# Gate and up projections as 2x2 block products: seven block products in place of eight, with weight sums on GpSimd

## The reference, cut to what matters

```python
x = x + concatenate([o_a, o_r]) @ w_out            # 1024 x 1024
h = rms_norm(x, g_ffn)
x = x + (silu(h @ w_gate) * (h @ w_up)) @ w_down   # 1024 x 2816, 1024 x 2816, 2816 x 1024
```

## Time and profile before

| what | value |
|---|---|
| median of 3 runs | 1565.37 us (1564.64 to 1566.42) |
| the profiled execution, its own time | 1564.63 us |
| its span, first to last instruction | 1563.1 us |
| PE busy | 1526.0 us (98%) |
| DVE busy | 737.0 us (47%) |
| ACT busy | 480.4 us (31%) |
| POOL busy | 43.3 us (3%) |
| mean granted TensorE clock | 0.998 |

### The profile page before, as it was taken

One profiled execution on the slowest core, in us unless ns is written; L12 is line 12 of the kernel. 1 busy time (PEld: TensorE's weight loads), 2 busy tenths in 40 slices (PEclk: granted clock), 3 DMA queues, 4 the chain that ended last, 5 costly groups with the idle time before them and its releaser, 6 DMA issues.

```text
span 1563.1 us, 29251 instructions
## 1 busy us (share of the span) xinstructions
PE 1526.0 (98%) x11565; PEld 1472.5 (94%) x11565; DVE 737.0 (47%) x1314; ACT 480.4 (31%) x740; POOL 43.3 (3%) x83
## 2 busy tenths in 40 slices
PE   6999999999999999999989999999999999999998
PEld 5998889999999999999989988898999999999998
DVE  5347754754444224443252777467544432344422
ACT  4233453443222112222232245434322221122211
POOL 1001100000000000000010010000000000000000
PEclk9999999999999999999999999999999999999999
DMA  5423321222223322223242133122222232222331
GB/s 175 118 68 106 93 62 58 71 80 79 81 81 96 93 60 86 83 86 93 64 136 82 55 123 91 42 67 81 73 81 81 81 107 73 77 81 81 96 91 62
DMA packets 220383, 132.50 MB, mean 85 GB/s; under 512 B 4424, under 2 KB 213504, under 8 KB 220304
## 3 DMA queue, kind: packets, MB, share of 16 engines
q1 hardware_dynamic: 215200, 114.11, 24.9%
q0 software_dynamic: 5008, 17.29, 3.6%
q10 hardware_dynamic: 96, 0.02, 0.0%
HBM read 123.23 MB, written 8.18 MB: 84 GB/s over the span
## 4 chain that ended last, share of the span: by engine, by line
PE 94%; DVE 3%; issue 2%; ACT 1%; DMA 0%; DVEq 0%; SPq 0%; ACTq 0%
PE ps L1134 70%; PE ps L1255 13%; PE ps L1309 2%; PE ps L1401 1%; PE ps L1416 1%; PE ps L1351 1%; PE ps L1331 1%; PE ps L1200 1%; PE ps L1180 1%; PE ps L1440 1%; DVE sc L905 0%; PE ps L1316 0%; DMA stage<-in_x_sample 0%; PE ps L1451 0%; DVE mix L923 0%
## 5 line engine op out<-in xcount | busy, mean ns | idle before, releaser
L1134 PE MATMUL ps<-ffn,w_hi 128*128 128x288 f32 x2816 | 489.7, 296 | 0.0
L1134 PEld LDWEIGHTS ps<-ffn,w_hi 128*128 128x128 f32 x2816 | 414.4, 189 | 0.2
L709 DVE TENSOR_TENSOR w_lo<-w_raw,w_hi 128x1024 fp32r<-128x1024 f32 (+1 forms) x192 | 247.7, 1290 | 171.6 <-ACT w_hi L439 171.6
L439 ACT ACTIVATE w_hi<-w_raw 128x1024 fp32r<-128x1024 f32 (+1 forms) x192 | 211.8, 1103 | 311.9 <-PE ps L1134 293.6
L1134 PE MATMUL ps<-ffn,w_lo 128*128 128x288 f32 x1408 | 301.6, 296 | 0.0
L1134 PE MATMUL ps<-act,w_hi 128*128 128x288 f32 x1408 | 244.6, 296 | 0.0
L1134 PE MATMUL ps<-mix,w_hi 128*128 128x288 f32 x1280 | 226.5, 300 | 12.1 <-DVE mix L723 10.2
L1134 PEld LDWEIGHTS ps<-ffn,w_lo 128*128 128x128 f32 x1408 | 226.9, 189 | 0.0
L1255 PE MATMUL ps<-mix,w_hi 128*128 128x288 f32 x1024 | 211.4, 300 | 0.0
L1134 PEld LDWEIGHTS ps<-act,w_hi 128*128 128x128 f32 x1408 | 207.3, 189 | 0.0
L1134 PEld LDWEIGHTS ps<-mix,w_hi 128*128 128x128 f32 x1280 | 190.8, 192 | 14.3 <-DVE mix L723 10.6
(11 more groups left out here) (183 smaller groups left out, 1113.1 us busy)
## 6 DMA issues: line engine op xcount, KB each, us to landing
w_raw<-in_w_in SPq DMA_DIRECT2D x56, 512.0 KB, 3.7
w_raw<-in_w_gate SPq DMA_DIRECT2D x44, 512.0 KB, 3.8
w_raw<-in_w_up SPq DMA_DIRECT2D x44, 512.0 KB, 3.8
w_raw<-in_w_down SPq DMA_DIRECT2D x32, 704.0 KB, 4.5
w_raw<-in_w_out SPq DMA_DIRECT2D x16, 512.0 KB, 3.6
strip_even<-bias_lines POOLq DMA_DIRECT2D x8, 320.0 KB, 4.4
strip_odd<-bias_lines POOLq DMA_DIRECT2D x8, 320.0 KB, 5.1
stage<-in_x_prompt SPq DMA_DIRECT2D x2, 1024.0 KB, 6.8
```

The lines of the kernel that those rows point to most:

```text
L439: nc.scalar.activation(w_hi[:, slot, 0:k, :], w_raw[:, slot, 0:k, :], ACT.Copy).then_inc(hi_done, 1)
L709: nc.vector.tensor_tensor(w_lo[:, slot, 0:k, :], w_raw[:, slot, 0:k, :], w_hi[:, slot, 0:k, :].bitcast(F32), ALU.subtract).then_inc(lo_don ...
L1134: last = nc.tensor.matmul(ps[:, bank + half, 0:HALF], w[:, slot, k, :], src[:, k, part, HALF * half:HALF * half + HALF], start=k == 0 and ...
```

## The change

The gate and up weights of block f form a 2x2 block matrix: rows gate and up, columns the two halves of the depth (4 blocks of 128 each). The activations form the other one: the two depth halves by the two token halves. Winograd's form of Strassen's method gets the four result blocks from seven block products: of A11, A12, A22 and four sums S1 to S4 of weight blocks, with B11, B21, B22 and four sums T1 to T4 of activation blocks. A block product is 4 depth blocks x 3 passes = 12 matmuls of 288 columns into one bank.

What each engine now does for one block f (a "pair"):

- SP loads both weights into `pair_raw` (two slots).
- POOL makes S1 = A21+A22, S2 = S1-A11, S3 = A11-A21, S4 = A12-S2 (`weight_sums`), each 128x512.
- ACT makes the high parts and DVE the low parts of the seven factors, each 128x512 (`factor_hi`, `factor_lo`). Each factor has a single place in SBUF; its next high part is made once its product is done (`follow`).
- PE runs the seven products in the order A11, A22 (of the pair before), S2, S1, A12, S3, S4. Some are added to what already lies in their bank.
- Between products ACT and DVE take partial sums out of PSUM: `product_1`, `made_15`, `made_16`, then the corners `corner_11`, `corner_12`, `corner_21`, `corner_22`. The products are not scaled one by one: `scale_gate` and `scale_up` use 576 columns.

In the layer's transition from `w_out`, the activation blocks and their sums are made and split (`operand`, `operand_sums`, `operand_lo`, `sum_lo`). The down units and the first part of the layer keep their work; buffers are placed anew.

The core of the diff (the helpers that only count are left out):

```diff
-        w_raw = place("w_raw", [P, RING, FT, P], F32, A_W)
-        w_hi = place("w_hi", [P, RING, FT, P], F32R, A_W + RING * UNIT)
-        w_lo = place("w_lo", [P, RING, FT, P], F32R, A_W + 2 * RING * UNIT)
+        FACTORS = ("A11", "S2", "S1", "A12", "S3", "S4")
...
+        BANK_1, BANK_5, BANK_6 = 4, 5, (3, 0)
+        FIRST_PAIR = ("A11", "S1", "A12", "S2", "S4", "S3")
+        STEPS = ("A11", "A22", "S2", "S1", "A12", "S3", "S4")
+        FACTOR_OF = {"A11": "B11", "A12": "B21", "A22": "T4", "S1": "T1", "S2": "T2", "S3": "T3", "S4": "B22"}
...
 (POOL)
+                        wait_apart(pool, (pair_loaded[n.par], pair_count(l, g, n)))
+                        free("S1", "S2")
+                        nc.gpsimd.tensor_tensor(w_sum["S1"][:], a21, a22, ALU.add).then_inc(w_summed, 1)
+                        wait_apart(pool, (w_summed, summed + n.count(4, 1)))
+                        nc.gpsimd.tensor_tensor(w_sum["S2"][:], w_sum["S1"][:], a11, ALU.subtract).then_inc(w_summed, 1)
+                        free("S3", "S4")
+                        nc.gpsimd.tensor_tensor(w_sum["S3"][:], a11, a21, ALU.subtract).then_inc(w_summed, 1)
+                        wait_apart(pool, (w_summed, summed + n.count(4, 2)))
+                        nc.gpsimd.tensor_tensor(w_sum["S4"][:], a12, w_sum["S2"][:], ALU.subtract).then_inc(w_summed, 1)
...
 (DVE; free() above waits for the low part of the last pair's factor of that name)
-                    with dve.Fori(1, FT - 1) as f:
-                        group_lo(2 * f + 1, 1)
-                        scaled(U_LAYER * l + 2 * f + first, 0, work[:, 0, :])
-                        act_low(f - 1)
-                        group_lo(2 * f + 2, 0)
-                        up_out(f)
-                        product(f)
+                    def steps(n):
+                        scale_gate(n.prev())
+                        follow(n, "A11")
+                        corner_21(n.prev())
+                        follow(n, "A22")
+                        made_16(n)
+                        follow(n, "S2")
+                        gate_up(n.prev())
+                        made_15(n)
+                        follow(n, "S1")
+                        scale_up(n.prev())
+                        follow(n, "A12")
+                        corner_22(n)
+                        follow(n, "S3")
+                        act_low(n.prev())
+                        corner_12(n)
+                        follow(n, "S4")
...
 (PE)
+                        for k in range(KH):
+                            for i, (w, part) in enumerate(PASSES):
+                                last = nc.tensor.matmul(ps[:, bank, 0:HALF], (f_hi, f_lo)[w][name][:, k, :], tile[:, at, k, part, :],
+                                                        start=start and k + i == 0,
+                                                        stop=k == KH - 1 and i == 2, skip_group_check=True)
+                        last.then_inc(products, 1)
...
+                    def steps(n, after_first=False):
+                        old, bank = n.prev(), BANK_6[n.par]
+                        product(n, "A11", n.at("A11"), BANK_1, True, (c11_out, done(n, 0)))
+                        corner_product(old, n.at("A22"))
+                        waits = [] if after_first else [(c21_made, done(n, -1))]
+                        product(n, "S2", n.at("S2"), bank, True, *waits)
+                        product(n, "S1", n.at("S1"), BANK_5, True, (c12_made, done(n, 0)))
+                        product(n, "A12", n.at("A12"), BANK_1, False, (p1_out, done(n, 1)))
+                        product(n, "S3", n.at("S3"), bank, False, (p16_made, done(n, 1)))
+                        product(n, "S4", n.at("S4"), BANK_5, False, (p15_made, done(n, 1)))
```

More of the change, by code:

```diff
@@ L684, in _, with follow @@
-                    with eng.Fori(1, FT - 1) as f:
-                        gate_up(f)
-                    silu(FT - 1)
-                    group_hi(DOWN, 0, FT)
-                    act_high(FT - 1)
-                    group_hi(DOWN + 1, 1, FT)
+                        sum_hi(2, slice(0, KH), 2 * KH)
+                    corner_11(first)
+                    def follow(n, name):
+                        m = n if name == "A22" else n.next()
+                        free = None if n.first and name == "A22" else (products, made + n.at(name) + 1)
+                        factor_hi(g, m, name, free)
@@ new lines, in corner_22, with corner_21 @@
+                    def corner_22(n):
+                        product_done(n, "S3")
+                        ours(p15_made, n)
+                        if not n.first:
+                            ours(act_f, n, 0)
+                        nc.vector.tensor_tensor(work[:, 1, HALF:TOK], ps[:, BANK_6[n.par], 0:HALF], p15_f[:], ALU.add).then_inc(c22_made, 1)
+                    def corner_21(n):
+                        dve.wait_ge(products, made + (n.next().at("A22") + 1 if n is not LAST else G_PROD))
+                        nc.vector.tensor_tensor(work[:, 1, 0:HALF], ps[:, BANK_6[n.par], 0:HALF], p1_f[:, n.par, :], ALU.add).then_inc(c21_made, 1)
@@ L1133, in passes @@
                     for half in range(2):
-                        last = nc.tensor.matmul(ps[:, bank + half, 0:HALF], w[:, slot, k, :],
+                        last = nc.tensor.matmul(ps[:, bank + half, 0:HALF], weights(w, slot, nk)[:, k, :],
                                                 src[:, k, part, HALF * half:HALF * half + HALF],
@@ L1527, in _, with corner_product @@
-                    unit(U_LAYER * l + first + DOWN, 0, FT, act, act_ready)
-                    unit(U_LAYER * l + first + DOWN + 1, 1, FT, act)
+                    first_product("S2", BANK_6[0], True, (evacuated, before + EV))
+                    first_product("S4", BANK_5, False, (p15_made, done(n, 1)))
+                    first_product("S3", BANK_6[0], False, (p16_made, done(n, 1)))
+                    if g == 0:
+                        rms_spread(l, 1)
+                    def corner_product(n, index):
+                        waits = [(c22_made, done(n, 1))]
+                        if n.first and g == 0:
+                            waits.append((b_lo, PARTS * l + NEEDS["A22"]))
+                        product(n, "A22", index, BANK_6[n.par], False, *waits)
@@ new lines, in _ @@
+                    steps(Pair(0, 1), after_first=True)
+                    steps(Pair(0, 2))
+                    with pe.Fori(1, FT // 2) as i2:
+                        for off in (1, 2):
+                            steps(Pair(i2, off))
+                    corner_product(LAST, G_PROD - 1)
+                    def act_ready(k):
+                        pe.wait_ge(act_lo, nth + k + 1)
+                    pe.wait_ge(c21_made, nth + FT - 1)
+                    unit(before, 0, FT, act, act_ready)
@@ L1529, in _ @@
+                    pe.wait_ge(c21_made, nth + FT)
+                    unit(before + 1, 1, FT, act)
                     with pe.Fori(1, U_OUT // 2) as c2:
@@ L1531, in _ @@
                         for s in range(2):
[L1532 removed]
+                            unit(U_LAYER * l + c + (FIRST_DOWN + U_OUT * g + s), s, FT, act)
             pe.wait_ge(evacuated, DEPTH * U_LAYER + EV)
```

547 lines of the change are left out of this document (429 added, 118 removed).

## The result

The change made the kernel slower: 1588.85 us (median of 4 runs, 1587.75 to 1590.02) against 1565.89 of the kernel before (4 runs, 1564.64 to 1566.87), a ratio of 1.0147 with a 95% interval of 1.013 to 1.0165. That is +23 us where +10.6 was forecast. The profiled execution's span went from 1563.1 to 1587.3 us, +24.2.

The account below looks back on a forecast made before the run. PE bounds the kernel before; DVE, blocked by POOL's sums, would bound the changed one. 1564.6 + 18.4 (36 rounds) - 12.8 (8 rounds) + 5.0 (transition) = 1575.2, forecast 1576 us, range 1497 to 1622.

Parts of the forecast that it names:

- PE's new pace: Gate/up loop: 84 matmuls a pair at 133 ns make PE's round 11.20 us, 1.60 less.
- the mechanism in the loop, with DVE as the new bound: Loop: POOL's sums block DVE, whose round becomes 13.31 us, 0.51 more than before; chance 0.60, of which 0.36 slower.
- the free case: Rival: POOL beside DVE costs nothing or nearly so, PE stays the bound, 1500 us as a median; chance 0.33.
- DVE's own list of 8.73 us: Loop: DVE's 16 operations a round, without blocking by POOL, take 8.73 us of PE's 11.20.
- 4.06 + 0.52 = 4.58 us a round: Loop: POOL's four sums cost DVE 4.06 us a round by blocking, four hand-overs 0.52 us.
- The first and last rounds of a group: 8 of 44 rounds, where DVE and POOL lack part of their work, run at PE's pace: -1.60 each, -12.8 us.
- the whole gain of 70.4 us: Loop: 1.60 us less of PE a round over 44 pairs, the most that can be gained there.
- in all I take 2.5 us a layer, 5 us in all (from 0 to 12): Transition from W_out: A12's late start and a second small wait before A22 cost 2.5 us a layer, 5 in all.
- A12's lateness: Transition: DVE comes late to the last chunk of x, so product A12 starts some 1.8 us late.
- The exclusion: POOL's sums and DVE's two-source SBUF instructions shut each other out; a sum costs DVE 1.20 or 0.83 us.
- Loaded about a round ahead; hidden: Weight loads: same bytes, 3.8 us from issue to landing for each half, issued about a round ahead, so no cost.
- The 0.37 us at each of 308 product starts: Rival: PE loses 0.37 us at each product's start, +114 us, 1614 instead of 1500; chance 0.07.

Follow-up runs that it names:

- kernel 1: Changed kernel with POOL's four sums left out and a constant written in place of S1 to S4: 1501.48 us, ratio 0.9582.
- kernel 2: Changed kernel with all four sums of every pair made on DVE and POOL idle: 1516.5 us, ratio 0.9682.
- kernel 6: Changed kernel with S1 and S2 on POOL, S3 and S4 on DVE, each group's first pair all on DVE: 1540.93 us, ratio 0.9837.
- experiment 8: Changed kernel with DVE making the sums of each group's first two pairs, POOL those of the other nine: 1580.19 us, ratio 1.0093.
- kernel 5: Changed kernel with POOL copying one raw block in place of each sum, the sums left out: 1506.71 us, ratio 0.9622.

## Why the prediction came out as it did

**Right: PE's new pace.** 84 matmuls at 133 ns: the rounds of kernels 1 and 2 are 11.1 us and PE is full.

**Right: the mechanism in the loop, with DVE as the new bound.** It was chosen over the free case although no row of before showed it, and experiment 1 confirms the choice: 87 us hang on what POOL reads and how long it does so. That the sign came out is less of a success: the prediction gave 0.43 to slower and 0.51 to faster. The rule of the Trainium skill ("SBUF - State Buffer", Who interferes with whom) predicted the two-source instructions' lengthening, that the later one waits for the other, and that PSUM sources are spared. The runs agree in all three (1.78 for 0.68 us; ends 0.55 to 0.61 us behind the sum's; 0.45 us).

**Sizes in the loop.** DVE's own list of 8.73 us holds: it gives 11.83 for the 11.8 of kernel 6, and 11.13 for kernel 2, where PE's 11.12 is kept. POOL's sum takes 1.28 us alone and 1.5 to 1.7 beside DVE, where I used 1.20. What it takes from DVE, forecast as 4.06 + 0.52 = 4.58 us a round, is 3.8. Why it is less isn't shown; likely part of a sum's time falls on DVE's PSUM operations, and part on POOL, which waits too. DVE also idles 0.4 us a round. A round is 12.93 against the forecast 13.31. The first and last rounds of a group are not each at PE's pace, as I had it: between the L1425 of the second group (599.60, 616.35 ... 718.16, 727.00) the first interval is 16.75 us and the last 8.84, together what two rounds of before took. In the first of them DVE waits for the third pair's late load. Against the kernel before, the loop is no better or worse, so that the whole gain of 70.4 us is gone; against kernel 1 it loses 19.6 us a group. The two errors, a round too long and edges too short, nearly cancel, which is luck: +1.0 a group where 9 x 0.51 - 2 x 1.60 = +1.4 was forecast, +4.0 us against +5.6 over four.

**The step that failed: "in all I take 2.5 us a layer, 5 us in all (from 0 to 12)".** The transition cost 20.2 us, 15 more than I had put down, and outside the bounds I gave it. The steps of it that went wrong:
- I priced A12's lateness at 1.8 us and stopped there. In kernel 2, where POOL does nothing, A12's wait is 2.29, A11 ahead of it waits 0.76, and 0.23, 1.58, 1.26 and 0.38 us follow, together 6.5 in the first layer; 2.15 of this stands in the second group as well. DVE is behind at the group's start and meets a list without slack for two pairs. A late engine must be followed until it has caught up.
- The exclusion that I charged in the loop I left out here. POOL's four sums fall on the preparation of a chunk of x (1.43 and 1.55 us for 0.5), and the second pair's four fall on what comes next. Experiment 8 takes both out: 20.2 becomes 12.8. Of this, 2.3 us go with the clock, which I had not counted at all: in layer 0 it stood at 0.50 behind A12's wait, and it didn't in experiment 8.
- "Loaded about a round ahead; hidden" was wrong too, though it is not what made the transition dear: the second groups have it as well. The load is issued once A22's low part of the pair in that buffer is made. The third pair's two, issued at 383.05 and 383.51, let ACT go on at 389.83. In the steady loop a load is issued at 447.07 and 447.55, the page gives 5.2 us from issue to landing for the second, and A11's high part starts at 453.24, half a microsecond later. It is just in time.

**The rivals.** The free case is what happens when POOL only writes (1501.48, forecast 1500), and what the changed kernel would be worth if its sums cost DVE less than the room it has. The 0.37 us at each of 308 product starts is nowhere: PE is busy for 70.00 of 70.00 us in kernel 1 with all of them. The order did what it said.

**What would have shown it.** In the loop these signs came as named: DVE over 90% busy (67.64 of 70), two-source operations well over 0.69 us, those from PSUM at 0.45, waits put down to low parts and DVE's results. The round of 13.3 us did not come (12.93 on the mean), and PE idled 1.5 us a round, not 2. I had named no sign for the transition, which is where most of the time went.

**Not settled.** What exactly makes up the 12 to 13 us that are left in every kernel. The late third pair is hardly a part of them: in kernel 2 the rounds behind DVE's first scaling take 11.11 to 11.13 us in the first groups as in the second. It leaves DVE's list ahead of that point: in kernel 2 PE waits 6.5 us for DVE in the first 45 us of the first group and 2.2 in as long a stretch of the second, and ACT waits only 0.8 us for a load. Kernel 1, where DVE makes no sums, has a first group of 128.7 us in layer 0 where kernel 2's is 131.5, both at the full clock there, so the list counts; what the rest of it costs is read from waits and not shown by an experiment. Why the clock fell in one layer and not in the other is also open, and why the third pair's load takes 5.2 us in some groups and 6.4 in others.

## What to carry to other kernels

Before work is moved to POOL, count what it takes from DVE: a two-source sum of 128x512 from SBUF cost DVE 0.9 to 0.95 us on POOL and 0.60 when DVE made it itself. With the sums on POOL the seven products lost 23 us against the kernel before, with the sums on DVE they gained 50 to 52. In these runs POOL's work cost nothing in the loop only where it read nothing (kernel 1) or where DVE had slack for it (kernel 5). When a schedule's steady round is right, walk through its first two rounds as well, engine by engine, with the same prices: here five sixths of the loss against the kernel before lay ahead of the loop. Measured against what seven products could give (kernel 1), the loop is the larger: 78 of 85 us.

## What the runs showed of the hardware

- POOL's reading of one stream (a copy of 128x512, 0.61 us at the least, 0.84 to 1.06 on the mean of each line) also lengthens DVE's two-source instructions, to 1041 ns on the mean for L1425, but writing alone (0.53 us for 128x512) doesn't: 754 ns.
- A one-source instruction of DVE is caught as well: TENSOR_SCALAR over 576 columns took 1.43 us beside a sum, and 0.51 in kernel 1.
- The granted clock fell to 0.50 (1.2 GHz) at PE's second wait, behind waits of 2.44 and 3.33 us in layer 0, and stood at 1.00 there when 24 matmuls filled the second. In layer 1 it read 0.50 for 3.4 us at the first wait (2.35 us) and 1.00 behind the second (3.08 us), so the lengths of the waits alone don't tell. Where it fell, the stretch took 23.97 us in place of 21.68; kernel 2 shows the same between its layers (24.27 and 21.92).
- The load of 512 KB that the first round waits for took 5.2 to 5.3 us in some groups and 6.3 to 6.4 in others, of the same program. A round that hangs on it moves by 1.1 us.
- A loop need not settle to one round: 12.2 and 13.7 us alternate in the changed kernel, where POOL's sums delay DVE.
